# Gather order of the expert rows in a two-layer-pair transformer forward pass: v of a group ahead of u of the next

## What is computed

```python
experts = jnp.take_along_axis(cand_i, best_pos, axis=-1).reshape(T, PEER_HEADS * PEER_TOPK)
gates = jax.nn.softmax(best_s, axis=-1).reshape(T, PEER_HEADS * PEER_TOPK)
...
act = jax.nn.gelu(jnp.einsum('td,ted->te', tb, expert_u[eb]).astype(jnp.float32), approximate=False)
return jnp.einsum('te,ted->td', (gb * act).astype(tb.dtype), expert_v[eb])
```

## Time and profile before

| | before |
|---|---|
| time, median of 3 runs | 2841.72 us (2838.48 to 2842.85) |
| the profiled execution | 2841.17 us, its span 2839.4 us |
| TensorE busy (matmul) | 2377.0 us, 84% |
| VectorE busy | 1510.5 us, 53% |
| GpSimd busy | 1166.3 us, 41% |
| ScalarE busy | 465.3 us, 16% |
| moved by DMA | 901.35 MB, mean 317 GB/s |

### The profile page before, as it was taken

How to read it: one execution, slowest core, us unless ns; L and a number is a source line. 1 busy time by engine, 2 the same in 40 slices (tenths; PEclk the granted TensorE clock), 3 DMA queues, 4 the chain that set the end, 5 groups by cost and what they waited for, 6 DMA issues and landing times.

```text
span 2839.4 us, 42235 instructions
## 1 busy us (share of the span) xinstructions
PE 2377.0 (84%) x17134; PEld 2203.0 (78%) x17134; DVE 1510.5 (53%) x3970; ACT 465.3 (16%) x972; POOL 1166.3 (41%) x1030
## 2 busy tenths in 40 slices
PE   7978899879889778889886867777777868999899
PEld 6877788778789778778786647777567867899699
DVE  0237578677478667577674655756646543111210
ACT  1211132101232101232111221002121002201210
POOL 0017657767567767656665223433223400000000
PEclk9989999889999889999997867887768988799799
DMA  7469999999999999999998647998548966367264
GB/s 283 168 270 396 412 366 382 412 383 406 413 396 414 411 373 400 415 379 376 412 367 326 225 174 282 406 350 337 214 176 322 415 242 253 127 250 292 77 242 157
DMA packets 179296, 901.35 MB, mean 317 GB/s; under 512 B 20732, under 2 KB 23840, under 8 KB 155936
## 3 DMA queue, kind: packets, MB, share of 16 engines
q0 software_dynamic: 147632, 537.47, 48.7%
q1 hardware_dynamic: 30608, 358.52, 32.0%
q10 hardware_dynamic: 864, 2.68, 0.2%
HBM read 897.53 MB, written 1.05 MB: 316 GB/s over the span
## 4 chain that ended last, share of the span: by engine, by line
PE 50%; DVE 19%; DMA 14%; POOL 8%; issue 7%; ACT 2%; DVEq 0%; SPq 0%; ACTq 0%; POOLq 0%
PE pa L803 23%; DMA vrow<-in_expert_v,idx 10%; DVE urow L1679 7%; PE ea L728 7%; PE pa L563 5%; POOL urow L2002 5%; DMA wring<-in_weights 3%; POOL vrow L2002 3%; PE pa L652 3%; DVE acc L1669 2%; PE pa L811 1%; DVE topi L1583 1%; PE pa L792 1%; PE pa L913 1%; PE s L589 1%
## 5 line engine op out<-in xcount | busy, mean ns | idle before, releaser
L2002 POOL DMA_INDIRECT urow<-in_expert_u,idx x512 | 604.1, 1180 | 908.1 <-DVE dots L1679 598.8
L728 PE MATMUL ea<-diag,vrow 128*128 128x128 f32 x4608 | 598.6, 295 | 174.6 <-DMA vrow<-in_expert_v,idx 173.6
L728 PEld LDWEIGHTS ea<-diag,vrow 128*128 128x128 f32 x4608 | 585.0, 211 | 189.8 <-issue 188.2
L2002 POOL DMA_INDIRECT vrow<-in_expert_v,idx x512 | 560.4, 1095 | 193.1 <-issue 151.4
L1679 DVE CUSTOM_DVE_ANT_0 urow<-urow,h2n 128x1024 f32<-128x1024 f32 x512 | 598.4, 1220 | 25.7 <-DMA urow<-in_expert_u,idx 24.7
L803 PE MATMUL pa<-hB,wring 128*128 128x144 f32 (+1 forms) x2496 | 348.3, 307 | 47.1 <-DVE gt L1968 23.4
L803 PEld LDWEIGHTS pa<-hB,wring 128*128 128x128 f32 x2496 | 343.0, 211 | 53.1 <-issue 34.7
L1669 DVE SCALAR_TENSOR_TENSOR acc<-vrow,wgt,acc 128x1024 f32<-128x1024 f32 x220 | 282.3, 1283 | 155.4 <-DMA vrow<-in_expert_v,idx 144.4
L563 PE MATMUL pa<-hA,wring 128*128 128x128 f32 x1536 | 177.8, 278 | 0.5 <-DVE hA L1457 0.5
L563 PEld LDWEIGHTS pa<-hA,wring 128*128 128x128 f32 x1536 | 176.0, 194 | 1.3 <-issue 1.3
L1220 ACT ACTIVATE gl<-dots 128x4 f32<-128x4 f32 x128 | 26.3, 205 | 843.5 <-DVE dots L1679 843.1
(11 more groups left out here) (340 smaller groups left out, 2704.7 us busy)
## 6 DMA issues: line engine op xcount, KB each, us to landing
wring<-in_weights SPq DMA_DIRECT2D x95, 2048.0 KB, 10.3
wlate<-in_weights SPq DMA_DIRECT2D x25, 2048.0 KB, 7.6
w<-in_weights SPq DMA_DIRECT2D x24, 2048.0 KB, 10.6
wring<-in_weights SPq DMA_DIRECT2D x22, 1408.0 KB, 8.4
wlate<-in_weights SPq DMA_DIRECT2D x10, 1408.0 KB, 6.8
urow<-in_expert_u,idx POOLq DMA_INDIRECT x512, 10.4
vrow<-in_expert_v,idx POOLq DMA_INDIRECT x512, 11.1
wring<-in_weights SPq DMA_DIRECT2D x3, 1792.0 KB, 10.8
```

The costliest lines, as they stand in the source:

```text
L728: m = pe.matmul(EA[c // 4][:, (c % 4) * P:(c % 4 + 1) * P], vrow[:, b, c * P:(c + 1) * P], diag[:, DIAG_SLOTS * (q % 2) + i, :], start=Fal ...
L2002: pool.indirect_dma_start(out=rows[:, b, :], out_offset=None, in_=table, in_offset=bass.IndirectOffsetOnAxis(ap=idx[:, k % 2, col:col + 1] ...
```

## The change

In GpSimd's list, the four v transfers of group q are asked for ahead of the four u transfers of group q+1; before, they stood behind them. The number, size and buffers of the transfers and what each waits for stay the same. No other engine's list changes.

```diff
             rows_u(0)
             for q in range(TURNS_E * GROUPS):
+                rows_v(q)
                 if q + 1 < TURNS_E * GROUPS:
                     rows_u(q + 1)
-                rows_v(q)
```

## The result

The changed kernel takes 2858.26 us, median of 9 runs (2846.25 to 2867.1), against 2839.97 us for the kernel before on the same occasions (9 runs, 2834.3 to 2848.22): ratio 1.0061, 95% interval 1.0037 to 1.0085. It is slower.

The account below looks back on a forecast made before the run. The prediction took the DMA, full from 200 to 1520 us, as the bound (ceiling 51 us); terms -9, -7.8, -3.6 and +6.4 summed to -14.0 us, giving 2827 us, range 2806 to 2856.

Parts of the forecast that it names:

- first-stage terms: First three units: dry places -9, attention stretches -7.8, unit changes -3.6, restarts on a dry queue +6.4 us.
- The last unit: Last unit of gathers: 0, since GpSimd's wait for dots covers later u rows; bounds 5 us less, 10 us more.
- v is 5.1 us earlier: Full queue: v has one block less in front, so TensorE's wait for it can end 5.1 us earlier.
- the three dry places: Places like 580 us, one in each of three units, with low DMA rate: 3 us gained each, -9 us.
- A later restart: GpSimd restarts 1.28 us later, behind VectorE's sum; free in a full queue, five restarts on a dry queue: +6.4 us.
- VectorE's path gets 1.2 us longer at these places, not 5.1.: VectorE's waits at the sum mostly become equally long waits for u; its path grows by one dot, 1.2 us.
- the prediction's last sign of being wrong: The prediction is wrong if the time changes but the last unit is where it does.
- The cover: Last unit: GpSimd's wait for dots, averaging 15.6 us, hides the later u rows.
- The slower rival: Late u's loop sets the pace if landing exceeds 13.6 us in most groups: +19, 2860 us, chance 0.25.
- No change: bytes decide: First stage: TensorE's gain before a dry place is VectorE's loss behind it; 2841 us, chance 0.19.
- either way: Forecast of 2827 us, whether taken from the profiled execution's 2841.2 us or the median 0.5 us above it.
- The port rule: VectorE's `tensor_scalar` can hold GpSimd's descriptor writes; eight restarts would cost 6 us more, sum 2833; not adopted.

Follow-up runs that it names:

- h_holdfirst: Kernel before, old transfer order, but in the first three units GpSimd waits for sum and matmuls of group q-2 ahead of the u rows of group q+1: 1.0050.
- b_first3: New order (v ahead of u) in the first three units only, old order in the last unit, against the kernel before: 0.9994.
- TensorE's part of the hold: Kernel before, old order; in the first three units GpSimd waits only for TensorE's matmuls ahead of the u rows: 0.9933 and 0.9957 on two slower chips.
- c_last: New order (v ahead of u) in the last unit only, old order in the first three units, against the kernel before: 1.0031.
- k_split: Kernel before, but in the first three units TensorE's three v rows go ahead of u, VectorE's fourth row behind with its sum wait: 0.9871, 0.9870, 0.9879.
- The hold on the sum alone: Kernel before, old order; in the first three units GpSimd waits only for VectorE's sum ahead of the u rows: 1.0122 and 1.0161 on two slower chips.

## Why the prediction was wrong

It said 2827 us, faster; measured are 2858 us, slower (1.0061, and 1.0037 in both repetitions). Two steps of the sum failed, and it takes both to turn the sign. The first-stage terms came to -2 us instead of -14, above all because the restart was put at 6.4 us where the hold costs 14. The last unit came to +8.8 us instead of 0. With only the second error the sum would still be -5 us, faster; with only the first it would be -2 us, no change. Both together give +7 us; the repetitions measured +10.5. Point by point:

- **"v is 5.1 us earlier", and the three dry places, -9 us.** Right in its place: TensorE's waits for v went, and the places are full. The gross gain of all the first-stage terms was put at 20.4 us; the difference of h_holdfirst and b_first3 is about 16.
- **"A later restart", +6.4 us.** This term was mis-sized. I counted five restarts of 1.28 us where the DMA is dry. The hold alone costs 14 us in the first three units. I had reasoned that a full queue makes the delay free; but the queue is only as full as GpSimd keeps it. The net is b_first3, 0.9994, -2 us instead of -14.
- **TensorE's part of the hold** I did not price at all: GpSimd's wait for TensorE grew from 5.6 to 70.4 us. On the slower chips this hold alone costs nothing (0.9933 and 0.9957). On the faster ones, where both holds together cost 14 us, it was not run alone, so its share there is open.
- **"VectorE's path gets 1.2 us longer at these places, not 5.1."** Too short. It forecast 100 to 150 us of waits for u, and 245.4 came. It left out that u is also asked for later; that this makes up the difference is argued, not shown.
- **The last unit: 0, between -5 and +10.** It came to 0.31%, 8.8 us, inside the bounds but not at 0, and the prediction's last sign of being wrong, that the last unit is where the time changes, came. The cover I named was the mean of GpSimd's waits over the whole unit, 15.6 us, against a delay of u rows by 10 to 12 us. But eight of its eleven waits from 1780 to 1930 and from 2170 to 2290 us are shorter than 10 us. The shortest are these, in the kernel before:

```profile
1836.18 1.74 POOL L2002 DMA_INDIRECT urow<-in_expert_u,idx  x1 [4.03 <-DVE dots L1679]
...
2234.59 1.74 POOL L2002 DMA_INDIRECT urow<-in_expert_u,idx  x1 [4.06 <-DVE dots L1679]
```

  The landing is longer there too: the row for which VectorE waited until 2238.60 us in c_last had been asked for at 2215.55, 23 us before, where the median from 200 to 1520 us is 11.0 us. The loss came from those 17 groups (1.0032), and hardly from the other 15 (1.0009).
- **The slower rival** (0.25, 2860 us) hit the time but not by its reason. Its point was a landing of over 13.6 us in most groups; the landing of u rows from 200 to 1520 us is

```profile
DMA to landing us min/median/max: 5.2/11.0/18.8
```

the same median as in the earlier trace rows, with a shorter tail. And it was priced for the first stage, which lost nothing net, with 29 us for the restarts where the hold costs 14. "No change: bytes decide" is what the first three units did in sum, though not because order is free there: h_holdfirst (1.0050) shows that it isn't, and k_split on the slower chips. The prediction's 2827 "either way" is 2827.7 from the median, a slip of no weight.
- **The port rule** of the Trainium skill (SBUF — State Buffer, section Who interferes with whom) would have made the first v issues longer, had they fallen on the `diag` instructions. They don't. At the place of the earlier trace rows the changed kernel has

```profile
581.82 0.68 DVE L1695 TENSOR_SCALAR diag<-kst,wgt 128x128 f32<-128x128 f32 x3
```

```profile
582.49 0.95 POOL L2002 DMA_INDIRECT vrow<-in_expert_v,idx  x1 [4.60 <-DVE acc L1669]
```

  and the 52 v issues that the sum released from 200 to 1520 us have a median of 0.94 us, where the 45 u issues that the dots had released before have 1.74. So the trace shows no such cost, and it doesn't test the rule. Nor were the old first issues long because of `diag`, as the prediction has it: the two issues of 1.74 us in the last unit, shown above, stand where VectorE makes no `diag`. The issue at 2234.59 lies beside its sum, which runs from 2234.24 to 2239.68.

## What to carry to other kernels

In a list that one engine works through in order, a wait belongs to everything behind it: price a reordering by whose wait now stands ahead of whom, separately from whose bytes come first. Here both effects were some 15 us in the first three units and cancelled. Moving only the instructions that can go without the sum's wait (three of four rows) gave 1.2 to 1.3% on three chips, of which 0.4 to 0.7% came already with GpSimd's wait for TensorE moved ahead. It was not run where the kernel before takes 2842 us, so its gain there is open. And a cover is to be read in the fullest stretch of a stage, not as a mean over the stage.

## What the runs showed of the hardware

The same kernel takes about 2842 us on some chips and 2966 to 2985 us on three others. The changed kernel has a profile on both kinds. Of the 167 us by which its span is longer on the third of these chips (3012.5 against 2845.1 us), 127 have come by the first dot of the last unit (1635.5 against 1508.7 us), 26 come in that unit and 14 behind it. The first stage on the third chip, columns as in the earlier trace rows:

```profile
200.00:1520.00 1320.00, 1079.65 (x7806) 991.00 (x7804) 841.32 (x2307) 229.77 (x450) 768.68 (x704) 0.89 0.94 361
```

It moves 361 GB/s at a share of 0.94, where the other chip moves 395 at 1.00. The hold on the sum alone costs more there (1.2 and 1.6%) than both holds cost on the faster chips (0.5%). Why these chips fall short, and why a hold on TensorE's matmuls gains 0.4 to 0.7% there, no run tells.

Full stretches of ten microseconds reached 429 GB/s at a share of 1.06, above the 412 that I took as full. The Trainium skill (DMA: Bandwidth & Descriptors, section Where 436 GB/s comes from) gives a limit of 435 GB/s, and the 10 us windows of the gathers shown here stay under it.
